# Delta-rule projection: its first four tiles from x times the norm weight, the norm's factor at the read from PSUM, and the entry of layer 0 in another order

## The reference

```python
for i in range(DEPTH):
    hn = rmsnorm(x, w['norm_mix'][i])        # x * rsqrt(mean(x*x) + eps) * g
    out, ... = mixer(hn, ...)                # i % 3 == 0: gdn_mixer
    x = x + out
    x = x + sqrelu_mlp(rmsnorm(x, w['norm_ffn'][i]), w['ffn_w1'][i], w['ffn_w2'][i])

def gdn_mixer(h, conv_buf, s0, w_in, conv_w, a_log, dt_bias, norm_w, w_out):
    proj = h @ w_in                          # 1024 x 4112: q, k, v (24 x 128), z (8 x 128), beta, a
    qkv, z, beta_pre, a_pre = split(proj)
    qkv, new_buf = causal_conv(qkv, conv_buf, conv_w)   # 4 taps along the tokens
    qkv = silu(qkv)
    ...
    g = -exp(a_log) * softplus(a_pre + dt_bias)
```

## Time and profile before

| | us |
|---|---|
| median of 3 runs (1619.77 to 1620.13) | 1619.87 |
| the profiled execution, its own time | 1616.97 |
| its span, first to last instruction | 1615.3 |
| granted TensorE clock over the span | 0.996 |
| PE busy | 1569.8 (97%) |
| DVE busy | 1046.2 (65%) |
| ACT busy | 877.6 (54%) |
| POOL busy | 250.2 (15%) |

### The profile page before, as it was taken

The page is one execution under the profiler, slowest core; times in us unless marked ns, Lnnn a source line. Parts: engine busy times, 40 slices in busy tenths (PEclk is TensorE's granted clock), DMA queues, the critical chain, the costliest instruction groups (busy, mean ns, idle before and its releaser), DMA issues.

```text
span 1615.3 us, 37803 instructions
## 1 busy us (share of the span) xinstructions
PE 1569.8 (97%) x16253; PEld 1485.3 (92%) x16253; DVE 1046.2 (65%) x1716; ACT 877.6 (54%) x1679; POOL 250.2 (15%) x319
## 2 busy tenths in 40 slices
PE   7999999999999999999999999999999999999997
PEld 6998799999997999999788888999999997999997
DVE  6965687754756877547583747775558837767643
ACT  4755656643645666434552546665347647666433
POOL 6005450000110200003003420200010026400000
PEclk9999999999999999999999999999999999999999
DMA  8951456555754655553624002665558623455550
GB/s 222 272 172 32 129 153 183 183 197 178 252 157 131 192 177 186 191 183 92 188 95 138 23 7 86 170 186 193 183 164 235 183 80 102 132 172 182 190 174 28
DMA packets 245530, 250.11 MB, mean 155 GB/s; under 512 B 16271, under 2 KB 239285, under 8 KB 245301
## 3 DMA queue, kind: packets, MB, share of 16 engines
q1 hardware_dynamic: 237040, 224.74, 45.7%
q0 software_dynamic: 8016, 22.86, 4.8%
q10 hardware_dynamic: 308, 0.10, 0.0%
HBM read 229.75 MB, written 18.32 MB: 154 GB/s over the span
## 4 chain that ended last, share of the span: by engine, by line
PE 90%; ACT 4%; DVE 4%; issue 1%; DMA 0%; DVEq 0%; SPq 0%
PE ps L806 86%; PE ps L810 4%; DVE acts L2631 1%; ACT st L1959 1%; ACT vk L1959 1%; ACT acts L1959 1%; ACT tri L1959 1%; DVE acts L2623 0%; DVE hn L2631 0%; DVE tri L2623 0%; ACT hn L1959 0%; DVE st L2631 0%; DMA acts<-in_x_sample_dram 0%; ACT w_gdn L1959 0%; PE ps L1727 0%
## 5 line engine op out<-in xcount | busy, mean ns | idle before, releaser
L2623 DVE TENSOR_TENSOR w_mlp<-ring,w_mlp 128x1024 fp32r<-128x1024 f32 x256 | 311.7, 1224 | 121.2 <-ACT w_mlp L1959 115.1
L1959 ACT ACTIVATE w_mlp<-ring 128x1024 fp32r<-128x1024 f32 x256 | 269.4, 1054 | 210.8 <-PE ps L806 210.8
L806 PE MATMUL ps<-hn_split,w_mlp 128*128 128x264 f32 x3072 | 373.3, 284 | 0.0
L806 PE MATMUL ps<-h_split,w_mlp 128*128 128x264 f32 x3072 | 372.6, 283 | 0.0
L806 PEld LDWEIGHTS ps<-hn_split,w_mlp 128*128 128x128 f32 x3072 | 372.0, 188 | 0.3
L806 PEld LDWEIGHTS ps<-h_split,w_mlp 128*128 128x128 f32 x3072 | 371.7, 188 | 0.0
L1959 ACT ACTIVATE tri<-ps 128x264 f32<-128x264 f32 (+4 forms) x226 | 103.3, 466 | 182.5 <-PE ps L806 156.3
L806 PE MATMUL ps<-gdn_hi,w_gdn 128*128 128x264 f32 x1024 | 195.0, 288 | 5.0 <-DVE mixer_lo L2623 4.4
L806 PEld LDWEIGHTS ps<-gdn_hi,w_gdn 128*128 128x128 f32 x1024 | 161.8, 190 | 9.3 <-issue 5.9
L806 PE MATMUL ps<-mixer_lo,w_gdn 128*128 128x264 f32 x512 | 146.1, 285 | 0.0
L2623 DVE TENSOR_TENSOR tri<-tri 128x264 f32<-128x264 f32 (+4 forms) x145 | 59.7, 413 | 101.3 <-ACT h_split L1959 100.6
(11 more groups left out here) (439 smaller groups left out, 2589.3 us busy)
## 6 DMA issues: line engine op xcount, KB each, us to landing
ring<-in_ffn_w_dram SPq DMA_DIRECT2D x128, 1024.0 KB, 5.4
ring<-in_gdn_w_in_dram SPq DMA_DIRECT2D x32, 1024.0 KB, 6.0
ring<-in_ml_w_in_dram SPq DMA_DIRECT2D x12, 1024.0 KB, 5.5
ring<-in_rw_w_rkv_dram SPq DMA_DIRECT2D x12, 1024.0 KB, 5.0
st<-in_state_gdn_S_dram POOLq DMA_DIRECT2D x2, 4096.0 KB, 23.2
ring<-in_gdn_w_out_dram SPq DMA_DIRECT2D x8, 1024.0 KB, 5.1
out_gdn_S_s_dram<-st SPq DMA_DIRECT2D x16, 512.0 KB, 4.4
st<-in_state_mlstm_C_dram POOLq DMA_DIRECT2D x1, 4096.0 KB, 19.9
```

The lines of the kernel that those rows point to most:

```text
L806: return nc.tensor.matmul(out, lhsT, rhs, start=start, stop=stop)
L1959: return nc.scalar.activation(out, in_, f, bias=bias, scale=scale)
L2623: return nc.vector.tensor_tensor(out, in0, in1, op)
```

## The change

In both delta-rule layers tiles 0 to 3 of the projection are made from x times the norm weight, split in a high and a low half (`gdn_raw`). DVE multiplies their results by `rstd` when it reads them from PSUM (`raw_tile`), into four spare tiles of `acts`, which then take the place of the banks. The norm's own sum is multiplied on PE behind tile 0 (layer 0: behind tiles 0 and 1). The normed activations are needed from tile 4 on and by the gate product, which moves behind tile 4. Weights run four parts ahead (`AHEAD`), on DVE five. Other small jobs move by two to three tiles: `gates` from behind the taps of tile 0 to those of tile 3, `gate_logs` from ACT's step 1 to step 4, `log_decays` from 2 to 5. In layer 3 ACT's and DVE's raw halves wait until the MLP's last matmuls have left the space they go to (`mlp_part`).

In layer 0 PE starts with three matmuls of 512 columns on ones, transposes the five large vectors first, sets a small matmul between the transposes of x and six of 256 columns behind them, and runs tiles 0 and 1 side by side (`abreast`), k by k. The eight smaller vectors go through SP's queue behind the second unit of weights. POOL takes over the adding of the squares, ahead of the masks.

```diff
-VEC_LOADS = 13
+VEC_LOADS = 8
+AHEAD = 4
...
+            def abreast(hi, lo, evac, ready, banks):
+                pe.wait_ge(wlo_ok, count.parts + UT)
...
+                for k in range(KT):
+                    pe.wait_ge(ready, count.seen(ready))
+                    for t in range(UT):
...
+                        mm(out, w_hi[:, k, :], hi[:, k, :], k == 0, False)
+                        mm(out, w_hi[:, k, :], lo[:, k, :], False, False)
+                        last = mm(out, w_lo[:, k, :], hi[:, k, :], False, k == KT - 1)
...
-                split_linear(gdn_hi, mixer_lo, 4 * D, lambda n: taps_ok if n < 24 else gdn_ev, hnl_ok, banks=4,
-                             hooks={0.5: gates, 0: conv_states, 3: log_decays_to_columns, 5: cumulate_decays, 11: sum_squares, 13: decay_exponents,
+                split_linear(gdn_hi, mixer_lo, 4 * D, evacuated, hnl_ok, banks=4, raw=gdn_raw[j], paired=not j,
+                             hooks={0.5: entry_norm, 0: conv_states, 2.5: gates, 4: log_decays_to_columns, 6: cumulate_decays, 11: sum_squares, 13: decay_exponents,
...
             pe.wait_ge(consts, count.seen(consts))
-            pe.wait_ge(x_in, count.seen(x_in, 48))
+            for _ in range(3):
+                mm(ps[6][:], ones[:], ones[:, 0:1].broadcast_to([P, 512]))
+            pe.wait_ge(consts, count.seen(consts))
+            pe.wait_ge(x_in, count.seen(x_in, 128))
+            tp(ps[7][:, 0:P], rowbuf(0, P, P)).then_inc(vec_T, count.up(vec_T))
...
+                if k < KT - 2:
+                    mm(ps[k + 1][:, 0:P], ones[:], ones[:])
...
+            for _ in range(6):
+                mm(ps[0][:, 0:UNIT], ones[:], ones[:, 0:1].broadcast_to([P, UNIT]))
...
+            def gdn_entry(j):
...
+                if j:
+                    gate_weights_hi(GH)
+                    ac.wait_ge(*mlp_part(i - 1, 1))
+                else:
+                    exp_ln_table()
+                    ac.wait_ge(vec_ok, count.seen(vec_ok))
+                for k in range(KT):
+                    if j and k == KT - 2:
+                        for _ in range(EARLY):
+                            weight_hi()
+                    if not j and k == 3:
+                        for _ in range(EARLY):
+                            weight_hi()
+                    ac.wait_ge(x_upd, count.seen(x_upd))
+                    raw_tile(k)
+                    if j or k < 3:
+                        square(k)
+                for k in range(3, 0 if j else KT):
+                    square(k)
+                for _ in range(EARLY, AHEAD):
+                    weight_hi()
+                if not j:
+                    gate_weights_hi(GH)
...
                 for n in range(32):
                     count.tiles += 1
-                    ac.wait_ge(lin_rdy, count.tiles)
-                    src = ps[n % 4]
+                    if n < RAW:
+                        ac.wait_ge(mx_ev, count.seen(mx_ev))
+                        src = acts[:, 3 * KT + n, :]
+                    else:
+                        ac.wait_ge(lin_rdy, count.tiles)
+                        src = ps[n % 4]
...
-                    if n < 32 - LEAD:
+                    if n < 32 - AHEAD:
                         weight_hi()
-                    if n == 1:
+                    if n == 4:
                         gate_logs()
                     if 2 <= n < 26:
                         silu_tile(n - 2)
...
+                    if i == 2 and n == FF // P - LEAD:
+                        gate_weights_lo(GH)
+                        dv.wait_ge(*mlp_part(i, 2))
+                        for k in range(KT - 2):
+                            gdn_raw_lo(1, k)
+                        for _ in range(EARLY):
+                            weight_lo()
...
+                def raw_tile(n):
+                    dv.wait_ge(lin_rdy, count.tiles + n + 1)
+                    tt(acts[:, 3 * KT + n, :], ps[n][:, 0:T], rstd[:, 1, :], ALU.mult).then_inc(mx_ev, count.up(mx_ev))
+
+                for _ in range(EARLY, AHEAD):
+                    weight_lo()
+                if not j:
+                    gate_weights_lo(GH)
+                norm(V_MIX + 3 * KT * j, gdn_hi, after={0: lambda: raw_tile(0), 5: lambda: raw_tile(1)})
+                raw_tile(2)
+                weight_lo()
...
                     last.then_inc(taps_ok, count.up(taps_ok))
                     weight_lo()
                     if n == 0:
+                        raw_tile(3)
+                        dv.wait_ge(mx_ev, count.own(mx_ev))
+                    if n == 3:
                         gates()
-                    if n == 2:
+                    if n == 5:
                         log_decays()
                     if n == 4:
                         conv_states()
```

More of the change, by code:

```diff
@@ L654, in hybrid_trunk, with mlp_part, gdn_part, vec2_rows @@
         parts = []
+        def mlp_part(i, kc):
+            return [part for part in parts if part[3] is w_mlp][2 * i * FF // P + FF // P + 6 * FF // P // 8 + 2 * kc + 1][2]
+        def gdn_part(j, n):
+            return [part for part in parts if part[3] is w_gdn][4 * KT * j + n][2]
+        def vec2_rows():
+            return acts[0:58, 3 * KT + 4, 0:P]
         def release(name, n):
@@ L1006, in conv_states @@
                             last = tp(ps[b][:, 24 * n:24 * n + 24], rowbuf(5, 24, 3 * D)[:, (12 * h + n) * P:(12 * h + n + 1) * P])
+                        if not j and not h:
+                            pe.wait_ge(vec_in, count.seen(vec_in, 16 * VEC_LOADS))
+                            last = tp(ps[b][:, 288:346], vec2_rows())
                         last.then_inc(conv_T, count.up(conv_T))
@@ L1984, in norm, with raw_tile, square @@
                     ac.wait_ge(x_upd, count.seen(x_upd))
                     act(sq[:, k, :], x[:, k, :], ACT.Square).then_inc(sq_ok, count.up(sq_ok))
-                for _ in range(1, early):
-                    weight_hi()
-                if not i:
-                    exp_ln_table()
                 ac.wait_ge(ms_mm, count.seen(ms_mm))
                 rsqrt(rstd[:, 1, :], rstd[:, 0, :], ps[1][:, 0:T], c(EPS), 1.0 / D, ms_ev, rstd_ok)
+            def gdn_entry(j):
+                i = 3 * j
+                raw_hi = gdn_raw[j][0]
+                def raw_tile(k):
+                    act(raw_hi[:, k, :], x[:, k, :], ACT.Copy, scale=vec1[:, V_MIX + KT * i + k:V_MIX + KT * i + k + 1]).then_inc(
+                        hnh_ok, count.up(hnh_ok))
+                def square(k):
+                    act(hn[:, k, :], x[:, k, :], ACT.Square).then_inc(sq_ok, count.up(sq_ok))
+                if j:
+                    gate_weights_hi(GH)
[20 more added lines that the diff above has]
+                    gate_weights_hi(GH)
+                ac.wait_ge(ms_mm, count.seen(ms_mm))
+                rsqrt(rstd[:, 1, :], rstd[:, 0, :], ps[7][:, 0:T], c(EPS), 1.0 / D, ms_ev, rstd_ok)
@@ L2120, in gdn @@
             def gdn(j):
-                if not j:
-                    weight_hi()
-                    gate_weights_hi(GH)
                 mixer_hi(gdn_hi)
-                for _ in range(LEAD - (EARLY if j else 1)):
-                    weight_hi()
                 def gate_logs():
@@ L2634, in copy, with norm @@
                 return nc.vector.tensor_copy(out, in_)
-            def norm(g, hi=None, first=False, after={}):
+            def norm(g, hi=None, after={}):
                 dv.wait_ge(rstd_ok, count.seen(rstd_ok))
@@ L2643, in norm @@
                         hn_ok, count.up(hn_ok))
-                    if first and k == 1:
-                        weight_lo()
-                        gate_weights_lo(GH)
                     if k in after:
@@ L2795, in conv_states @@
                         dv.wait_ge(conv_T, count.seen(conv_T))
+                        if not j and not h:
+                            copy(vec2[:], ps[4][:, 288:346])
                         copy(swin[:, 12 * h:12 * h + 12, :, 0:3],
@@ L2864, in gdn @@
                 sample_conv(16, 24)
-                for n in range(24, 31 - LEAD):
+                for n in range(24, 30 - AHEAD):
                     weight_lo()
```

148 lines of the change are left out of this document (92 added, 56 removed).

## The result

The changed kernel takes 1633.67 us (median of 4 runs, 1632.24 to 1639.51), the kernel before beside it 1619.82. The ratio is 1.0102, with a 95% interval of 1.009 to 1.0115: 1.0% slower. The forecast was 1623.2, slower by 0.2%, so the sign was right and the size was not. The profiled execution has a span of 1632.6, which is 17.3 more than the one of before.

What follows compares the result with a forecast made beforehand. PE, busy for 97% of the span, bounds the kernel, with DVE close behind. Layer 3 +0.9 and layer 0 +2.4 give +3.3, so the median goes from 1619.87 to 1623.2; range 1614.5 to 1628.

Steps and rivals of the forecast that it cites:

- I take the early rise: Layer 0: about 5 of matmuls on ones and the transposes raise the clock by 10, so layer 0's sum holds.
- the rival's 20.5: Layer 0: clock rises late, at 20.5, and tile 10 ends 4.6 later; total 1627.8, chance 0.18.
- sign of being wrong: Layer 0: PEclk still at 0.50 at 15 would show the forecast wrong.
- at nothing as long as x is there by about 8.5: Layer 0: loading the vectors in the wait for x costs nothing if x arrives by about 8.5.
- a stall of 5.4: Ahead of tile 9: PE waits from 33.4 to 38.8 behind ACT's and DVE's queued work, 5.4 lost.
- six low halves at a pitch of about 0.45: Layer 3 entry: DVE makes six raw low halves at about 0.45 each; with two low weights they end at -0.5.
- wait of 0.8 at tile 10: Tile 10 waits for taps 6, behind low weight 10 and log_decays: 0.8 more lost.
- one table holds Exp and Ln: Rival: one table load of 1.28 less in each layer, -2.6, total 1620.6; chance 0.22.
- longer loads: Rival: four exposed table loads each have a tail of 1.38, +5.5, total 1628.7; chance 0.04.
- the forecast had 0.9: Layer 3 ends 0.9 later: 7.6 of new waits in place of a hole of 6.8.
- no stall: Rival: the stall at tile 9 does not form, 6.2 less per layer, total 1610.8; chance 0.20.
- The 0.5 ahead of tile 4: Layer 3, first stall: PE waits from 15.5 until DVE reaches its first taps at 16.0, 0.5 lost.

Runs made afterwards that it cites:

- c3_l3_best_warm: Kernel before with layer 3's part alone, its three small changes (later gate_logs, table set asked for, POOL's sum earlier), and layer 0's warm-up only: ratio 0.9960.
- b1: Kernel before with the change made in layer 3 alone, layer 0 and the kernel's start as they were: ratio 1.0032.
- b2: Kernel before with the change in layer 3 alone, plus gate_logs and log_decays later, the table set asked for and POOL's sum earlier: ratio 0.9969.
- a3_pool_first: Changed kernel with POOL's adding of the squares in layer 3 moved ahead of its wait for the MLP's space: ratio 1.0073 to the kernel before.
- a1_late_logs: Changed kernel with gate_logs moved from ACT's step 4 to 6 and log_decays from tile 5 to 7: ratio 1.0063 to the kernel before.
- a2_table_asked: Changed kernel with ACT asking for the table set of Exp and Ln ahead of gate_logs' first Exp: ratio 1.0076 to the kernel before.
- a4: Changed kernel without its first three matmuls of 512 columns on ones: ratio 1.0113 to the kernel before.
- c2: Changed kernel with later gate_logs, table set asked for, POOL's sum earlier and longer warm-up, without the six wide matmuls on ones: ratio 0.9987 to the kernel before.
- a5_fill_stall: Changed kernel with three matmuls of 512 columns on ones between tiles 8 and 9, by mistake also in layer 1: ratio 1.0082 to the kernel before.

## Why the prediction was wrong in size

**The step that failed first** is "I take the early rise", with the sentence ahead of it that a warm-up and the transposes raise the clock by 10. The clock did rise at 5.7 and fell again at 9.2; the rise that lasted came at 22.8, later than even the rival's 20.5. The forecast's own sign of being wrong, a clock of 0.50 at 15, is what the trace shows. Measured: 5.3 of layer 0's 10.2 (the longer warm-up gives it back). The order on ACT and the table set are the rest: with them layer 0 goes from 4.9 to -1.0. I had asked when the clock rises, and not whether PE stays busy. The wait for the vectors, which the forecast costed "at nothing as long as x is there by about 8.5", set PE idle for 2.44, and the earlier work on ones was lost. x came at 8.65, just as assumed. The weights did not bind; PE's own transposes and fillers did.

The reading behind that step was off too. The forecast says that 10 of transposes and norm did not raise the clock before the change. In the trace that it read they did, with a rise at 17.3 and a fall at 20.7, behind an idle time of 3.91:

```profile
20.43 0.36 PE L806 MATMUL ps<-gdn_hi,w_gdn 128*128 128x264 f32 x1 [3.91 <-DVE mixer_lo L2623]
20.62 0.38 PE L806 MATMUL ps<-mixer_lo,w_gdn 128*128 128x264 f32 x1
```

The two starts are 0.19 apart. At half speed, in c3_l3_best_warm, the same two are 0.36 apart (20.34 and 20.70). In b1 and b2, with the same code there, they are 0.35 and 0.36 apart, so this rise is there in one execution and not in another. The trace of before thus held the very thing that the change then met: a clock that an idle time takes away.

**What the sum lacked** is the clock behind the stall at tile 9: 1.7 in layer 3 by itself. In layer 0 the same fall is seen (0.50 at 64 to 67), but its price there was not separated from the other effects. The forecast priced a stall of 5.4 as 5.4. None of its rows shows the clock fall in mid-kernel, and behind the entry of layer 0 the clock of before stays up until the last 8 us. But the sentence that it quotes from TensorE: Matmul & The Clock Gate, "What's actually happening", in the Trainium skill has two sides, and I used one: if throttled is the default state, a long idle time must bring it back. The runs agree, and this should have been a rival.

**A mis-sized term:** "six low halves at a pitch of about 0.45". They took 0.83, as POOL's adds run beside them. It cost about 2.3 of layer 3's 4.8 (a3_pool_first). The row that I took it from the earlier trace rows is a single low half with POOL idle. The six in the same stretch were in the trace too, x6 in 5.08 with POOL's five adds beside them, and I had not read them. The GPSIMD Engine Reference of the Trainium skill, section "Specifications", says that POOL's SBUF interface is shared with VectorE and that the two contend when a DVE instruction has two SBUF inputs; the runs agree: 0.83 beside POOL's adds, and 3.38 for all six where only the first two had them beside, which leaves (3.38 - 2 x 0.83) / 4 = 0.43 for one alone, an estimate from these rows.

**What held.** The mechanism of the stall at tile 9, its place, its four table loads and its size (5.0 and 5.1 for 5.4). The cause was shown by moving gate_logs. The wait of 0.8 at tile 10 is there (0.74) once the clock is up. One load is 1.3, and "one table holds Exp and Ln" and "longer loads" fall: the rows at 54.53 and 55.83 are 1.30 apart. In layer 3, 4.8 less 2.3 for POOL and 1.7 for the clock leaves 0.8, where the forecast had 0.9. That takes for granted that the two prices add, which no run shows; some luck may be in it. DVE's first taps stood 18.0 behind PE's freedom and not 16, and in a3_pool_first `rstd` is 2.1 earlier. The side that I gave 0.20, no stall, did not come, but a1_late_logs shows what it is worth in layer 3: a gain. The 0.5 ahead of tile 4 was not there in layer 3; in layer 0 PE idled 2.85 there.

**Between the layers.** Of the 2.4 there, 1.6 arise in layer 1, where the profile after reads 0.50 from 545.0 to 548.5 and that of before has no low clock. The other profiles settle what this is. In a2_table_asked, with the same code in layer 1 and no low clock there, the 1.6 are absent, and what lies between the layers takes as long as before. So they are the clock's, not the change's work. Such a stretch in layer 1 stands in six of the fifteen new profiles, also in c3_l3_best_warm, and one between 183 and 201 in four (a1, a3, a4, c2).

**Open.** What decides whether the clock falls in one execution and not in the next stays open, and so does the price of the fall at tile 9 in layer 0.

## What to carry to other kernels

- Ask of every wait that is moved what stands behind it on its engine. Here a small job of 6 in ACT's order, three steps later than before, held up a weight that a third engine needed, and moving it two steps further paid 5.8 in one layer.
- A stall of PE has a second price, the matmuls behind it at half speed. A warm-up pays only if it reaches to the first real work: 5.1 of it with 2.44 of idle time raised the clock and lost it again, and were worth nothing; 6.3 with 0.76 were worth 5.3.
- Take a pitch from a row with the same neighbours, not from the one instruction that ran alone.

## What the runs showed of the hardware

- PEclk ahead of its first recorded change is no reading. At 1.00 six passes of 512 columns took 5.14 (0.86 each) at the start of the changed kernel, and ten took 4.47 (0.45 each) in the filled stall. With no warm-up (a4) PE began at half speed and the first record was the rise at 20.4.
- The clock fell behind idle times of PE of 3.91, 2.5, 2.44, 2.04 and 1.86, and held behind 0.76 and 0.69. Behind the 2.8 to 3.2 ahead of tile 4 in layer 0 it fell in nine of twelve profiles (in that of the longer warm-up, for one) and held in three (in that of the changed kernel, for one). In a5_fill_stall it fell also at 1220.7, amid waits of 1.01, 0.54 and 1.26 behind which it held in the changed kernel. So a short idle time is a risk and no fixed price. In a1_late_logs the granted clock (0.987 against 0.991 to 0.993) goes with a time 5 to 10 longer.
- POOL's adds of 264 columns beside DVE raised DVE's pitch for a low half from 0.43 to 0.83, and two low weights from 2.35 to 2.90.
